# A two-layer decoder trunk with product-key experts: VectorE and ScalarE take a unit's step of the woven front ahead of that unit's dot and diagonal

## What is computed

```
def peer_ffn(xn, wq, subkeys, u, v):
...
        s = jnp.einsum('thcd,hcnd->thcn', q, subkeys).astype(jnp.float32)
        s1, i1 = lax.top_k(s[:, :, 0], K)
        s2, i2 = lax.top_k(s[:, :, 1], K)
...
        top_s, pos = lax.top_k(cand, K)
        eidx = jnp.take_along_axis(cidx, pos, axis=-1)
        g = jax.nn.softmax(top_s, axis=-1)
        ue = u[eidx]
        ve = v[eidx]
        act = jax.nn.gelu(jnp.einsum('td,thkd->thk', xi, ue).astype(jnp.float32), approximate=False)
        return jnp.einsum('thk,thkd->td', (g * act).astype(ve.dtype), ve)
```

## Time and profile before

| | |
|---|---|
| timed, median of 3 (lowest, highest) | 1705.8 us (1703.42, 1705.91) |
| the profiled execution: its time, its span | 1704.57 us, 1702.5 us |
| bytes moved by DMA | 670.05 MB, of which 536.90 MB by the 512 gathers |
| busy: TensorE, VectorE, ScalarE, GpSimd | 79%, 58%, 42%, 36% of the span |
| granted clock of TensorE, mean | 0.854 of 2.4 GHz |
| ACT_TABLE_LOAD on ScalarE | 60 + 23, 1283 ns each |

### The profile page before, as it was taken

How to read it: one execution, slowest core, us unless ns; L and a number is a source line. 1 busy time by engine, 2 the same in 40 slices (tenths; PEclk the granted TensorE clock), 3 DMA queues, 4 the chain that set the end, 5 groups by cost and what they waited for, 6 DMA issues and landing times.

```text
span 1702.5 us, 24065 instructions
## 1 busy us (share of the span) xinstructions
PE 1346.4 (79%) x8582; PEld 695.8 (41%) x8582; DVE 990.6 (58%) x2463; ACT 719.9 (42%) x1992; POOL 607.8 (36%) x516
## 2 busy tenths in 40 slices
PE   7997999887898769777787669787788577666776
PEld 6776865553564126343453116344354111111111
DVE  0351767774557845744556865764558964444444
ACT  2232247555523433654532444653533443333333
POOL 0000132433433333233423443232334455555562
PEclk9998999988999979998898679998899675676666
DMA  9516799999999999999999999999999999999997
GB/s 380 213 58 234 302 416 412 420 413 421 422 422 423 420 422 422 422 423 422 421 419 420 421 405 422 422 421 422 422 421 385 422 421 423 421 421 421 421 421 301
DMA packets 88872, 670.05 MB, mean 394 GB/s; under 512 B 9632, under 2 KB 14128, under 8 KB 15664
## 3 DMA queue, kind: packets, MB, share of 16 engines
q0 software_dynamic: 73728, 536.90, 76.2%
q1 hardware_dynamic: 15024, 131.61, 18.9%
HBM read 667.43 MB, written 1.05 MB: 393 GB/s over the span
## 4 chain that ended last, share of the span: by engine, by line
DMA 42%; PE 36%; DVE 11%; issue 4%; ACT 4%; POOL 2%; SPq 0%; POOLq 0%; DVEq 0%; PEldq 0%; ACTq 0%
DMA arena<-in_experts,idxT 42%; PE psum L597 35%; DVE arena L1655 6%; POOL arena L2074 2%; ACT cst L1085 1%; DVE red L1624 1%; ACT gains L1085 1%; DVE cst L1616 1%; ACT ring L1085 1%; DMA ring<-in_ev_sq 1%; ACT L1085 1%; ACT gelus L1085 0%; DVE cst L1622 0%; PE psum L980 0%; DVE rstd L1547 0%
## 5 line engine op out<-in xcount | busy, mean ns | idle before, releaser
L2074 POOL DMA_INDIRECT arena<-in_experts,idxT x512 | 607.5, 1187 | 1071.5 <-PE psum L597 820.9
L597 PE MATMUL psum<-arena,cst 64*64 64x512 f32 (+1 forms) x4102 | 687.6, 757 | 287.4 <-ACT cst L1085 286.7
L1655 DVE CUSTOM_DVE_ANT_0 arena<-arena,xrow 128x1024 f32<-128x1024 f32 x512 | 622.3, 1224 | 501.6 <-DMA arena<-in_experts,idxT 499.1
L1085 ACT ACTIVATE gelus<-red 128x1 f32<-128x1 f32 x512 | 103.4, 202 | 735.4 <-DVE red L1655 734.3
L597 PEld LDWEIGHTS psum<-arena,cst 64*64 64x64 f32 (+1 forms) x4102 | 131.1, 155 | 683.3 <-ACT cst L1085 605.1
L597 PEld LDWEIGHTS psum<-hT,ring 128*128 128x128 f32 x2304 | 276.7, 197 | 116.5 <-issue 109.6
L597 PE MATMUL psum<-hT,ring 128*128 128x128 f32 x2304 | 298.8, 286 | 24.1 <-DVE hT L1499 19.5
L1085 ACT ACTIVATE cst<-cst,gains 128x128 f32<-128x128 f32 x512 | 206.3, 403 | 17.8 <-PE psum L597 0.8
L1085 ACT ACTIVATE gains<-gelus,gateT 128x1 f32<-128x1 f32 x512 | 150.8, 295 | 17.0
L597 PEld LDWEIGHTS psum<-mixT,ring 128*128 128x128 f32 (+1 forms) x592 | 71.3, 196 | 28.2 <-issue 23.8
L597 PE MATMUL psum<-mixT,ring 128*128 128x128 f32 (+1 forms) x592 | 78.2, 286 | 3.8 <-issue 3.1
(11 more groups left out here) (226 smaller groups left out, 851.8 us busy)
## 6 DMA issues: line engine op xcount, KB each, us to landing
ring<-in_pq SPq DMA_DIRECT2D x15, 2048.0 KB, 11.6
ring<-in_ev_out SPq DMA_DIRECT2D x4, 2048.0 KB, 10.2
ring<-in_xq SPq DMA_DIRECT2D x4, 2048.0 KB, 11.5
ring<-in_xo SPq DMA_DIRECT2D x4, 2048.0 KB, 11.6
arena<-in_experts,idxT POOLq DMA_INDIRECT x512, 15.6
ring<-in_od_out SPq DMA_DIRECT2D x4, 2048.0 KB, 12.0
ring<-in_ev_sq SPq DMA_DIRECT2D x2, 2048.0 KB, 8.9
ring<-in_ev_sk SPq DMA_DIRECT2D x2, 2048.0 KB, 13.0
```

Source lines behind the costliest of these rows:

```text
L597: return nc.tensor.matmul(out, lhsT, rhs, start=start, stop=stop)
L1085: return nc.scalar.activation(out, in_, f, **k)
L1655: V.tensor_tensor_reduce(out=ut, in0=ut, in1=xrow[:, u // PAIRS, :], scale=1.0, scalar=0.0, op0=ALU.mult, op1=ALU.add, accum_out=dots[:, k ...
L2074: nc.gpsimd.indirect_dma_start(slot[slot_of(u)], None, d["experts"], bass.IndirectOffsetOnAxis(ap=idxT[:, u:u + 1], axis=0))\
```

## The change

On VectorE and ScalarE the step of unit u (clock u + 1) is now called ahead of unit u's dot and diagonal, as on TensorE, for all units but the first. What `experts` adds itself behind a dot (`softmax`, `route_early`, `add_back`) or a diagonal (`rows_out`) stays there, so that it now comes behind the step instead of ahead of it.

```
@@ scalar
                 for k in range(PAIRS):
                     u = t * PAIRS + k
                     r = u % SLOTS
+                    if l or u:
+                        clock[0] = l * UNITS + u + 1
+                        for f in fronts:
+                            next(f, None)
                     if l == t == 0 and k in GATES_AT:
                         exponentials(*EARLY_HEADS[GATES_AT[k]], GATES_AT[k])
                     act.wait_ge(dotted, l * UNITS + u + 1)
...
                     if closed and k == BACK_LAG:
                         rows_out(*closed[-1], closed[-2] if len(closed) > 1 else None)
-                    clock[0] = l * UNITS + u + 1
-                    for f in fronts:
-                        next(f, None)
+                    if l == u == 0:
+                        clock[0] = 1
+                        for f in fronts:
+                            next(f, None)
@@ vector
                 for k in range(PAIRS):
+                    if l or t or k:
+                        clock[0] = l * UNITS + t * PAIRS + k + 1
+                        for f in fronts:
+                            next(f, None)
                     unit(l, t * PAIRS + k)
...
                     if closed and k == BACK_LAG + 4:
                         add_back(*closed[-1])
-                    clock[0] = l * UNITS + t * PAIRS + k + 1
-                    for f in fronts:
-                        next(f, None)
+                    if l == t == k == 0:
+                        clock[0] = 1
+                        for f in fronts:
+                            next(f, None)
```

## The result

The changed kernel takes 1709.63 us in the median of 20 runs (1706.38 to 1714.53), the kernel before 1705.41 us in 20 runs beside it (1700.71 to 1709.4). The ratio is 1.0026, 95% interval 1.0019 to 1.0033: by the ratio 4.4 us slower (4.2 us between the medians), more than the 3.4 us that a measurement here tells from no change. Forecast were 1706 us and no change; the time lies in the range, but on the side to which I gave 0.15, and by a mechanism that was none of my rivals. What they explain is the loss of the lower one, 2.8 us; where the upper one comes from stays open.

The account below looks back on a forecast made before the run. The prediction took the DMA as the bound from 190 us on. From the profiled 1704.57 us, less 0.9 and plus 1.2, came 1704.9; with 1.23 for the timed median 1706.1, said as 1706, range 1701.5 to 1710.5.

Parts of the forecast that it names:

- The bound: From 190 us to the last gather the DMA bounds at 421 or 422 GB/s; at most 7.8 us can be won.
- the price of such a place: Where the DMA runs short, the loss is the stretch's length times the rate missing against 421 GB/s.
- 350 to 370 us: Projection of step 47 and the gather behind it come sooner: a gain of 0.9 us, bounds 0 and 1.0.
- 190 to 350 us: Mostly TensorE, busy 149 of 160 us in unchanged order: 0 taken, 1.9 us as the bound of a gain.
- The cover: Gathers land 15.6 us after issue in the median, so dots or diagonals late by a few us only shorten a queue.
- My last sentence: Most wrong if ScalarE, waiting for TensorE's jobs ahead of a diagonal, keeps TensorE waiting in a chain not followed; no size.
- rival (b): A drain at table loads on ScalarE's path is real, so 0.9 us is not won: 1707.0 us, chance 0.07.
- 1280 to 1310 us: Dot 351 queues behind VectorE's wait for scores and gathers go out later: a loss of 1.2 us, bounds 0 and 2.5.
- the sign that I had named: If right, 1280 to 1320 us would show lower GB/s, by the equal of 1 to 2 us.
- The other stretches: VectorE's busy stretches at 960 to 1000 us and around 580: 0 taken, bounds -0.5 and +2.5 us.
- (c): Dots behind steps lose a ring place where VectorE is busy: 2.5 us in each of three stretches, 1712.4 us, chance 0.15.
- (d): TensorE's same-beat waits emptied the queue, so 4.2 us is won and nothing lost at 1300: 1701.6 us, chance 0.11.

Follow-up runs that it names:

- e2: Changed kernel with the step ahead only in units 26 to 43, all others as in the kernel before: 1709.54 us, ratio 1.0022 to the kernel before.
- e10: Changed kernel with the step ahead only in units 26 to 33, all others as in the kernel before: 1706.5 us, ratio 1.0009 to the kernel before.
- e14: Changed kernel with the step ahead only in units 44 to 60, all others as in the kernel before: 1706.13 us, ratio 1.0003 to the kernel before.
- e5: Changed kernel with the step ahead only from unit 340 on, all others as in the kernel before: 1706.5 us, ratio 1.0003 to the kernel before.
- e6: Changed kernel with the step ahead only in units 44 to 339, others as in the kernel before: 1705.62 us, ratio 0.9995 to the kernel before.
- e15: Kernel before, but all generators except gla ahead in units 26 to 43 and all ahead in 44 to 339: 1705.2 us, ratio 0.9998.
- e12: Changed kernel with the step ahead only in units 26 to 43 without unit 28, others as in the kernel before: 1706.55 us, ratio 1.0001.
- e13: Changed kernel with the step ahead only in units 26, 27 and 28, others as in the kernel before: 1705.98 us, ratio 1.0005.

## Why the prediction was right and where it was wrong

*The bound.* Right: the DMA holds 421 to 422 GB/s in the long stretches, and only places where the queue runs empty count. I had also given the price of such a place, length times missing rate; for e2 it gives 4.9 us lost and 1.0 won from 350 to 370 us, for a measured 3.8. For e10 the two windows (406 and 409 GB/s) give 3.8 less 0.4, for a measured 1.5 (0 to 3.1), so it is a rough price.

*190 to 350 us.* This is the step that failed: "mostly TensorE, 149 of 160 us busy, in unchanged order. I take 0, and 1.9 us as the bound of a gain." An engine that is busy 93% of the time in unchanged order still starts late where what it waits for is moved, and the bound had only one side. The pieces were in the trace of before. The cover that I used everywhere, 15.6 us to landing, was a median of the whole span, where 290 to 350 us had medians of 11.3 to 13.3 us. The 5.9 us of exponentials and table loads and the level waits (2.9 us, behind the dot) were not followed, while I did follow a step of the same kind at 350 us and at 1300 us. My last sentence, on ScalarE keeping TensorE waiting in a chain not followed, named half of it; the other half is VectorE's wait for TensorE ahead of a dot, the pattern that I had priced at 1296 us.

*350 to 370 us.* Right in e14, where nothing ahead disturbs it: the table load expected at 345.0 started at 345.30, the root expected at 347.6 was ready at 347.85, the projection expected at 351 started at 352.10, since the matmuls of unit 45 ahead of it took 1.99 us and not 1 (the granted clock from 350.2 to 352.2 us was 0.50, 1.2 GHz); the gather expected at 356 to 357 went at 356.57. In the changed kernel the same chain came later (the gather at 358.75 after 3.44 us of GpSimd's wait, against 360.33 and 7.75), because of what had gone on before it. The window rose to 423 GB/s as forecast, but since e2 has 422 there without the moved chain, that sign showed nothing. And the drain of rival (b) is not there: the load at 345.30 is followed at 346.59, 1.29 us later. The Trainium skill, ScalarE: Activation LUTs, section What ACT_TABLE_LOAD costs, gives some 2.66 us for the switch with its drain, and by an estimate from that the function would have started at about 347.96. The trace has 346.59, and the measurement decides.

*1280 to 1310 us.* The order of events was right; in the changed kernel GpSimd issues at

```profile
1303.31 0.94 POOL L2084 DMA_INDIRECT arena<-in_experts,idxT  x1 [1.27 <-PE psum L597]
1304.92 0.99 POOL L2084 DMA_INDIRECT arena<-in_experts,idxT  x1 [0.68 <-issue]
1308.09 0.94 POOL L2084 DMA_INDIRECT arena<-in_experts,idxT  x1 [2.17 <-PE psum L597]
1309.42 1.98 POOL L2084 DMA_INDIRECT arena<-in_experts,idxT  x1 [0.40 <-issue]
1314.23 0.94 POOL L2084 DMA_INDIRECT arena<-in_experts,idxT  x1 [2.83 <-PE psum L597]
```

where I had said 1303.2, 1305.2, 1308.0, 1309.4 and 1314.4 (the earlier trace rows for before). The size is in agreement: e5 loses 1.5 us by the gathers, for the 1.2 us taken; its time, 0.0003 or 0.5 us, can neither show nor exclude that. The window of this stretch itself rose from 371 to 416 GB/s in the changed kernel, since the queue was deeper on entering (from 1260 to 1280 us the median to landing is 18.4 us, 13.8 in the kernel before). e14 has 18.1 us and 398 GB/s there with the order of before in this stretch, so the rise is not made by this stretch's order, and the sign that I had named, a lower rate from 1280 to 1320 us, could not be read from the changed kernel.

*The other stretches and the rivals.* (c) asked for 2.5 us each around 580, 960 and 1280 us; e6 (0.9995) excludes the first two. It had the right sign for a wrong place and a wrong mechanism, 6.6 us where 4.4 were measured. That the measured time lies in the range owes something to luck: the range ended at 1710.5 us for other reasons, and the loss in it had been priced nowhere. (d), 4.2 us faster, is excluded by e6 and e15, and by e14 what is won at 350 us is too small to measure. 62 table loads came as forecast.

*Open.* What the 7 slower of the changed kernel's 20 runs have in common was not found; no run of e2 went over 1711.75 us.

## What to carry to other kernels

Before a step is moved ahead of a producer's work, list for every step what it waits for and how long it runs, and hold this against the depth of the queue at that very place; a median over the whole run hides the stretch that has no cover. "Busy and in unchanged order" is no reason for a zero, and a term without a followed chain needs a bound on both sides. Where two delays lie behind each other, the first may cost only the cover and the second the time, so that each alone looks free; e12 and e13 suggest this and do not show it. The time from issue to landing is a rough gauge of that depth, as e10 shows.

## What the runs showed of the hardware

The granted clock at the very end differs between executions of kernels that have the same order there: the same 16 matmuls took 2.04 us at a granted 1.00 and 3.77 us at 0.50, and with the unit ahead of them (1.16 and 2.06 us) that is 2.6 us of the span that the order there does not decide; a single profiled pair can't be compared to better than that here. On ScalarE a function follows the start of a table load after 1.29 us (345.30 to 346.59), with no further gap.
